# The last of 32 experts: its down piece in two column halves, its outputs added 32 rows at a time, another order of its products and transfers, and stores on two DMA queues

## The reference

```python
x = x + g1[:, None] * mix
h = rms_norm_2(x, norm2_g[l]) * (1.0 + sc2[:, None]) + sh2[:, None]
y = hierarchical_moe(h, w_rg, b_rg, w_re, b_re, w_gate, w_up, w_down)
x = x + g2[:, None] * y
return rms_norm_2(x, final_g)
```

## Time and profile before

| | |
|---|---|
| median of 3 runs | 916.79 us (915.58 to 919.57) |
| the profiled execution | 915.51 us |
| its span in the profile | 913.5 us |
| instructions | 13147 |
| busy share: PE, PE weight loads, DVE, ACT, POOL | 85%, 51%, 41%, 19%, 4% |
| moved from HBM | 282.75 MB |

### The profile page before, as it was taken

How to read it: one execution, slowest core, us unless ns; L and a number is a source line. 1 busy time by engine, 2 the same in 40 slices (tenths; PEclk the granted TensorE clock), 3 DMA queues, 4 the chain that set the end, 5 groups by cost and what they waited for, 6 DMA issues and landing times.

```text
span 913.5 us, 13147 instructions
## 1 busy us (share of the span) xinstructions
PE 773.8 (85%) x5441; PEld 466.3 (51%) x5441; DVE 373.0 (41%) x881; ACT 170.1 (19%) x473; POOL 39.6 (4%) x36
## 2 busy tenths in 40 slices
PE   7999899999998999998999996858767676677675
PEld 4544664456577644466477573535534444345332
DVE  2478678557854676537342322111111111121113
ACT  3222631213356310023120000000000000001001
POOL 1110000023300000000000000000000000000000
PEclk9999999999999999999999998999889999799779
DMA  9983507665003659972969999999999999999994
GB/s 344 395 310 130 185 1 272 235 231 184 1 1 134 224 159 379 396 298 77 382 254 411 426 427 429 428 429 429 428 428 429 427 430 429 427 430 429 424 430 174
DMA packets 54556, 284.40 MB, mean 311 GB/s; under 512 B 2800, under 2 KB 7280, under 8 KB 41968
## 3 DMA queue, kind: packets, MB, share of 16 engines
q1 hardware_dynamic: 54512, 283.81, 77.5%
HBM read 282.75 MB, written 1.05 MB: 311 GB/s over the span
## 4 chain that ended last, share of the span: by engine, by line
PE 57%; DMA 33%; DVE 4%; ACT 2%; issue 2%; POOL 1%; SPq 1%; DVEq 0%; POOLq 0%
DMA ring<-in_up_w 30%; PE banks L1800 15%; PE banks L1934 15%; PE banks L2298 8%; PE banks L1884 3%; DMA ring<-in_down_w 2%; PE banks L2346 2%; PE banks L1832 2%; PE banks L2283 2%; PE banks L1869 1%; PE banks L1912 1%; POOL rs L577 1%; PE banks L1778 1%; DVE soft L1070 1%; ACT probs L651 1%
## 5 line engine op out<-in xcount | busy, mean ns | idle before, releaser
L2298 PE MATMUL banks<-ring,QT 128*32 128x256 f32 x1696 | 143.8, 449 | 61.2 <-DMA ring<-in_up_w 61.2
L1934 PE MATMUL banks<-ring,hT 128*128 128x512 f32 (+4 forms) x384 | 157.2, 564 | 1.4 <-DMA ring<-in_ab_w 1.2
L1800 PE MATMUL banks<-ring,hT 128*128 128x512 f32 x320 | 139.9, 594 | 2.5 <-issue 1.5
L2298 PEld LDWEIGHTS banks<-ring,QT 128*32 128x32 f32 x1696 | 72.6, 124 | 110.1 <-DMA ring<-in_up_w 44.5
L1934 PEld LDWEIGHTS banks<-ring,hT 128*128 128x128 f32 x384 | 72.1, 192 | 74.3 <-issue 65.9
L1696 DVE TENSOR_TENSOR QT<-banks,MOD 32x256 f32<-32x256 f32 x128 | 53.8, 420 | 132.8 <-PE banks L2346 131.5
L1800 PEld LDWEIGHTS banks<-ring,hT 128*128 128x128 f32 x320 | 60.1, 190 | 78.9 <-issue 73.8
L1687 DVE TENSOR_TENSOR QT<-QT,banks 64x256 f32<-64x256 f32 x32 | 13.5, 423 | 195.2 <-ACT QT L919 195.2
L2346 PE MATMUL banks<-ring,QT 128*32 128x256 f32 x992 | 61.4, 387 | 14.9 <-ACT QT L926 12.4
L577 POOL TENSOR_TENSOR rs<-st,mhalf 128x1 f32<-128x1 f32 (+7 forms) x27 | 32.4, 1203 | 867.8 <-DVE st L1733 448.1
L919 ACT ACTIVATE QT<-banks 64x256 f32<-64x256 f32 x32 | 12.0, 375 | 292.2 <-PE banks L2298 292.2
(11 more groups left out here) (353 smaller groups left out, 712.8 us busy)
## 6 DMA issues: line engine op xcount, KB each, us to landing
ring<-in_up_w SPq DMA_DIRECT2D x30, 2048.0 KB, 23.7
ring<-in_down_w SPq DMA_DIRECT2D x30, 2048.0 KB, 21.9
ring<-in_gate_w SPq DMA_DIRECT2D x23, 2048.0 KB, 20.4
ring<-in_ada_w SPq DMA_DIRECT2D x12, 2048.0 KB, 15.3
probs<-in_gate_w SPq DMA_DIRECT2D x8, 2048.0 KB, 29.3
ring<-in_ab_w SPq DMA_DIRECT2D x4, 2048.0 KB, 19.8
ring<-in_cd_w SPq DMA_DIRECT2D x4, 2048.0 KB, 13.6
ring<-in_in_w SPq DMA_DIRECT2D x4, 2048.0 KB, 14.3
```

Of the source, the lines that this page charges most:

```text
L1800: ins = pe.matmul(bank[j % 4][:, 0:n], hT[:, k, t * P:(t + 1) * P], w[:, k, :], start=(k == 0), stop=(k == KD - 1))
L1934: ins = pe.matmul(bank[b][:, 0:n], hT[:, k, t * P:(t + 1) * P], w[:, k, :], start=(k == 0), stop=(k == KD - 1))
L2298: return pe.matmul(bank[1][CAP * j:CAP * j + CAP, 0:256], XG[:, k, CAP * s:CAP * s + CAP], wk[:, :, 2 * (j % 2):2 * (j % 2) + 2], start=(k ...
```

## The change

- **Transfers.** The loop runs on to the last expert, so the order becomes G30, U30, D30, G31, U31, D31. D31 comes in two halves of 512 columns (all four row chunks), each with its semaphore.
- **Order on TensorE.** Expert 31's gate_up follows down(30). Between its gate and its up products stand the additions of experts 28 to 30 (`add_outputs(7)` with 96 rows).
- **Down products of 31.** `down_last(half)`: for each column half 16 matmuls of 128 columns, in strips n = 0 to 3, into bank 0 or 1. Strip n gets columns 128n to 128n + 127 of the half. VectorE multiplies the 128x128 result once by the gate row, laid out in strips before (`outputs_last`, `gate_strips`).
- **Additions of 31.** `add_last(half)`: eight matmuls with 32 weight rows (one row strip each), 128 weight columns and 128 streamed ones, in two turns of four. A turn uses four row strips and four banks and waits for the turn before it. The weights are SW's last 32 columns, repeated four times and turned (`spread_last` at expert 24, two more transposes and a copy at 28).
- **Layout of the sums.** The banks of a token tile hold quarter columns: bank b has columns 256b to 256b + 255 of each half. Residual, additions and YE are read in that order.
- **The end.** ScalarE waits for all 16 sums and squares 128x1024 at once for each token tile; VectorE orders the two means and four row blocks by hand; SyncE stores column half 0 and ScalarE column half 1.

The diff, without the branch for crowded experts, which isn't run here:

```diff
+        def by_bank(a):
+
+            return a.rearrange("p (h b n) -> p b h n", h=2, b=2)
...
+        def sum_bank(t, b):
+            return bank[4 + 2 * t + b][:, :].rearrange("p (h n) -> p h n", h=2)
...
+        def sum_half(t, h):
+            return banks[:, 4 + 2 * t:6 + 2 * t, 256 * h:256 * h + 256]
...
+        gate_strips, last_out = [MOD[:, 1, 256 * i:256 * i + 256].rearrange("p (h n) -> p h n", h=2) for i in range(2)]
+        last_spread, last_spreadT = [MOD[:, 2, 256 * i:256 * i + 256].rearrange("p (t n) -> p t n", t=NT) for i in range(2)]
...
-                for e in range(6, NE - 2):
-                    for j in range(1 if e == 6 else 0, 3):
+                for e in range(6, NE):
+                    for j in range(1 if e == 6 else 0, 2 if e == NE - 1 else 3):
                         once_in_four = e % 2 == 0 and j == 0
                         load_gathered(3 * (e % 2) + j, e, e - 4 if once_in_four else e - 2)
-                for e in (NE - 2, NE - 1):
-                    for j in range(2):
-                        load_gathered(3 * (e % 2) + j, e, e - 4 if e % 2 == 0 and j == 0 else e - 2)
-                load_gathered(2, NE - 2, NE - 4)
                 sp.wait_ge(*upto("g_down", NE - 2))
                 down = srcs[2](NE - 1)
                 for half in range(2):
-                    sp.dma_start(ring[eslot(5)][:, 2048 * half:2048 * half + 2048].rearrange("p (k n) -> p k n", k=2),
-                                 down[:, 2 * half:2 * half + 2, :]).then_inc(sem(f"last_down{half}"), 16)
+                    sp.dma_start(ring[eslot(5)][:, 2048 * half:2048 * half + 2048].rearrange("p (k n) -> p k n", k=FC),
+                                 down[:, :, 512 * half:512 * half + 512]).then_inc(sem(f"last_down{half}"), 16)
...
-                for c in range(2):
-                    sp.wait_ge(*upto("out", 2 * t + c + 1))
-                    sp.dma_start(out[t * P:(t + 1) * P, 512 * c:512 * c + 512], X[:, t, 512 * c:512 * c + 512])\
-                      .then_inc(sem("st"), 16)
+                sp.wait_ge(*upto("out", 2 * t + 1))
+                store(sp, t, 0)
...
-                for b in range(4):
-                    act.wait_ge(*upto("sums", b + 1))
-                    sumsq(bank[4 + b][:, :], st[:, b:b + 1], "sum_ss", Y[:, b // 2, D + 512 * (b % 2):D + 512 * (b % 2) + 512])
+                act.wait_ge(*upto("sums", 16))
+                for t in range(NT):
+                    sumsq(banks[:, 4 + 2 * t:6 + 2 * t, :], st[:, t:t + 1], "sum_ss", in_halves(Y[:, t, D:2 * D]))
...
+            for t in range(NT):
+                act.wait_ge(*upto("out", 2 * t + 2))
+                store(act, t, 1)
...
+                if last_quad(q):
+                    v.tensor_copy(last_spreadT, bank[0][:, 256:512].rearrange("p (t n) -> p t n", t=NT))
...
+            def spread_last():
+
+                v.wait_ge(*upto("g_sw", QUADS))
+                v.tensor_copy(by_expert(last_spread), SW[:, :, 3 * CAP:4 * CAP].unsqueeze(2).to_broadcast([P, NT, 4, CAP]))\
+                 .then_inc(sem("g_swr"), 1)
+                for n in range(4):
+                    strip = slice(CAP * n, CAP * n + CAP)
+                    ins = v.tensor_copy(gate_strips[strip, :, :],
+                                        MOD[strip, 5, :].rearrange("p (h s n) -> p s h n", h=2, s=4)[:, n, :, :])
+                ins.then_inc(sem("g_swr"), 1)
+
+            def outputs_last(half):
+
+                v.wait_ge(*upto("g_down", NE + half))
+                if half == 0:
+                    v.wait_ge(*upto("g_swr", 2))
+                v.tensor_tensor(last_out[:, half, :], bank[half][:, 0:P], gate_strips[:, half, :], ALU.mult)\
+                 .then_inc(sem("g_ye"), 1)
 
...
-                    if e < NE - 1:
-                        hidden(e)
-                    if e == NE - 2:
-                        hidden(NE - 1)
+                    hidden(e)
                     if e % 4 == 0:
                         turned(q)
                         if q + 1 < QUADS:
                             select(q + 1)
                             spread(q + 1)
-                    outputs(e)
-                for t in range(NT):
-                    o = slice(2 * t, 2 * t + 1)
-                    v.wait_ge(*upto("sum_ss", 2 * t + 2))
-                    go(v.tensor_scalar(st2[:, t:t + 1], st[:, o], st[:, 2 * t + 1:2 * t + 2], D * EPS, ALU.add, ALU.add), "ms")
-                    rooted()
-                    for c in range(2):
-                        cols = slice(512 * c, 512 * c + 512)
-                        v.scalar_tensor_tensor(out=X[:, t, cols], in0=bank[4 + 2 * t + c][:, :], scalar=rs[:, t:t + 1],
-                                               in1=MOD[:, 0, cols], op0=ALU.mult, op1=ALU.mult).then_inc(sem("out"), 1)
+                        if q + 1 == QUADS - 1:
+                            spread_last()
+                    if e < NE - 1:
+                        outputs(e)
+                for half in range(2):
+                    outputs_last(half)
+
+                def final_mean(t):
+                    v.wait_ge(*upto("sum_ss", t + 1))
+                    means(1, 1.0, a=t, eps=D * EPS)
+
+                def final_rows(t, c):
+                    cols = slice(512 * c, 512 * c + 512)
+                    v.scalar_tensor_tensor(out=in_halves(X[:, t, cols]), in0=sum_half(t, c), scalar=rs[:, t:t + 1],
+                                           in1=in_halves(MOD[:, 0, cols]), op0=ALU.mult, op1=ALU.mult).then_inc(sem("out"), 1)
+
+                final_mean(0)
+                rooted()
+                final_rows(0, 0)
+                final_mean(1)
+                final_rows(0, 1)
+                rooted()
+                final_rows(1, 0)
+                final_rows(1, 1)
...
                             strip(k, j)
+                    add_outputs(q)
                     gathered_landed(pe, q, s, 1)
...
-                    gathered_landed(pe, q, s, 2)
+                gathered_landed(pe, q, s, 2)
                 pe.wait_ge(*upto("g_hc", e + 1))
                 if last_quad(q):
...
-                        pe.wait_ge(*upto(f"last_down{c // 2}", 16))
                     a = 64 * (c % 2) + CAP * (c // 2)
                     for n in range(4):
                         ins = pe.matmul(bank[2][CAP * n:CAP * n + CAP, 0:256], HG[:, a:a + CAP],
                                         wd(c)[:, 256 * n:256 * n + 256], start=(c == 0), stop=(c == FC - 1))
                 ins.then_inc(sem("g_down"), 1)
 
...
+            def down_last(half):
+
+                if half == 0:
+                    pe.wait_ge(*upto("g_hc", NE))
+                pe.wait_ge(*upto(f"last_down{half}", 16))
+                for c in range(FC):
+                    a = 64 * (c % 2) + CAP * (c // 2)
+                    at = 2048 * half + 512 * c
+                    for n in range(4):
+                        ins = pe.matmul(bank[half][CAP * n:CAP * n + CAP, 0:P], HG[:, a:a + CAP],
+                                        ring[eslot(5)][:, at + P * n:at + P * n + P], start=(c == 0), stop=(c == FC - 1))
+                ins.then_inc(sem("g_down"), 1)
+
+            def add_last(half):
+
+                pe.wait_ge(*upto("g_ye", NE + half))
+                for turn in range(2):
+                    if half + turn > 0:
+                        pe.wait_ge(*upto("sums", 8 * half + 4 * turn))
+                    for t in range(NT):
+                        for b in range(2):
+                            n = 2 * b + (t + turn) % 2
+                            strip = slice(CAP * n, CAP * n + CAP)
+                            at = 256 * half + P * (n % 2)
+                            pe.matmul(bank[4 + 2 * t + b][:, at:at + P], last_spreadT[strip, t, :], last_out[strip, half, :],
+                                      start=False, stop=half + turn == 2, tile_position=(CAP * n, 0)).then_inc(sem("sums"), 1)
+
...
+                if last_quad(q):
+                    pe.wait_ge(*upto("g_swr", 1))
+                    for t in range(NT):
+                        ins = pe.transpose(bank[0][:, 2 * P + P * t:3 * P + P * t], last_spread[:, t, :], ident)
                 ins.then_inc(sem("g_swt"), 1)
...
-            def add_outputs(q, last=False):
-
+            def add_outputs(q):
+
+                experts = 3 if last_quad(q) else 4
+                some = slice(0, CAP * experts)
                 pe.wait_ge(*upto("g_swc", q + 1))
-                pe.wait_ge(*upto("g_ye", q * 4 + 4))
+                pe.wait_ge(*upto("g_ye", q * 4 + experts))
                 for j in range(4):
-                    ins = pe.matmul(bank[4 + j][:, :], SWT[:, j // 2, :], YE[:, 512 * (j % 2):512 * (j % 2) + 512],
-                                    start=False, stop=last)
-                    if last:
-                        ins.then_inc(sem("sums"), 1)
-                if not last:
```

(15 more changed lines are left out.)

## The result

The changed kernel takes 920.31 us (median of 20 runs, 918.88 to 922.98), the kernel before 917.47 (20 runs, 915.44 to 921.5). The ratio is 1.0029, with a 95% interval of 1.002 to 1.0039: slower by 2.8 us, too little to pass the 0.5% set in the prediction. Forecast were 2.8 us and "about the same". The profiled executions lie further apart, 919.84 and 915.51; e5 to e11 show a part of why.

What follows compares the result with a forecast made beforehand. Expert weight transfers bound the kernel until about 880, so the last 33 us decide. Additions +1.1 and a longer end +1.7 gave +2.8 us, put on the median 916.79: 919.6 us, range 916.0 to 922.5.

Steps and rivals of the forecast that it cites:

- the 0.5% set in the prediction: Whole kernel: smallest difference told from no change, about 0.5% or 4.6 us, from runs reaching 915.58 to 919.57.
- The transfers: Last weight pieces: expert 30's down lands 885.6, expert 31's gate 890.4, up 895.3, down 899.9 including 0.4 for 2 KB runs.
- Up to the hidden rows: Expert 31 on TensorE: gates from 890.8, 3.3 us; additions 3.67, 2.5 on the path; up 3.3, ending 901.1.
- Down products and turns: Expert 31: down halves 0.93 us each, then four turns of 32-row additions at 0.72 each; last sum 908.0, +1.1 us.
- the second rival: Expert 31's additions: row strips don't overlap, a turn costs 1.3 us, total 921.9; decides from about 1.2; chance 0.15.
- The rule of the Trainium skill on serialized increments: Expert 31's additions: increments on every packed matmul serialize, 26.3 ns each, an estimated 0.4 us more, 920.0 in the end.
- The factor for four row strips: Expert 31's additions: four row strips at 3.07 times one, an estimated 0.6 us a turn, 0.5 us less in all.
- The end: Squares, means and row blocks: last sum to last row 5.2 us, 1.7 more than 3.5, as all banks close together.
- The store: After the last rows: last store lands 3.07 us later, kept from before, as each last store has a free queue.
- Additions at no cost: Rival at expert 31's up products: set by the up piece's landing alone, all after 2.5 us earlier, 917.1; chance 0.15.
- An order that doesn't show: Rival on transfers: expert 30's down piece lands one piece late, 890.4, its products 1.6 us later, 921.2; chance 0.05.
- A gain: Whole kernel: faster by more than 4.6 us; nothing reaches it, as up can't end before 898.6; chance 0.05.

Runs made afterwards that it cites:

- e5: The kernel before, unchanged, traced once more for its scatter: 916.63 us, last rows to end 3.06 us.
- e11: The kernel before, unchanged, for a third trace of the granted clock: last rows to end 2.5 us, clock 0.51 in the last additions; no total time given.
- e1: Changed kernel with the additions of experts 28 to 30 between gate and up of expert 31 left out: ratio 1.0006, median 918.11 us.
- e2: Changed kernel with the additions of experts 28 to 30 moved behind expert 31's down products, ahead of the 32-row additions: ratio 1.0049.
- e7: Kernel before with only the new end (squares of 128x1024 after all sums, new order of means and row blocks), one queue: ratio 1.0027.
- e3: Changed kernel with all four stores on SyncE's queue again: ratio 1.005.
- e6: Kernel before with column half 1 stored from ScalarE's queue and nothing else: ratio 1.0014.
- e4: Changed kernel with the earlier order of transfers and products, additions of experts 28 to 30 behind the down halves: ratio 1.0027.
- e9: Kernel before with ten idle matmuls on TensorE in the waits before expert 31's down products and the last additions: ratio 0.9994, median 917.06 us.
- e8: Kernel before with earlier additions of experts 28 and 29, outputs of 30 and 31 added in strips, new end, two queues: ratio 1.001.
- e10: The kernel before with strip additions for experts 30 and 31 and the new end, but all stores on SyncE's queue: ratio 0.9986, median 915.64 us.

## Why the prediction came out

**The transfers.** Right in order and time: gates at 891.07 for 890.4 (the stream was 0.7 late as a whole), down(30) without a wait. D31 landed at 901.17 for 899.9. The 0.4 us for its 2 KB runs was near: it lands 5.1 to 5.2 us after the piece ahead of it in the five kernels with column halves, 4.9 in the eight with row halves, so 0.2 to 0.3. Of the 1.3 us that it came later than forecast, 0.7 is the later stream, and 0.7 comes from taking the end of the bytes, 899.5, for the landing, 900.18. All of it stayed hidden here, as the products came at 904.38.

**Up to the hidden rows.** The mechanism is shown by e1 and e2. Two terms were mis-sized: gates and up were each put at half of 6.58, 3.3 us; apart they take 3.82 and 3.77, because each is a full run of its own and nothing of one runs beside the other. Before, the last of the gates and the first of the ups ran side by side: 18 records are at work between 891.1 and 891.9, 10 between 889.6 and 890.4. So splitting them costs 1.0 us in itself, whatever stands between. With the gates' start 0.4 late, up ends at 902.43 for 901.1.

**Down products and turns.** Halves 1.96 together for 1.86; four turns 2.6 us for 2.9. The row strips overlap; the second rival is out, since it needed 1.2 us a turn and the longest was 0.62. The rule of the Trainium skill on serialized increments ("TensorE: Matmul & The Clock Gate", "The cost: per-tile semaphore tail") has no 0.4 us to show here: all four turns came out below the sum without it. No run leaves the increments out, so the rule itself isn't tested. The factor for four row strips in the Trainium skill (same page, "Measured speedup vs the span model") fits better: the estimate from it was 0.6 a turn, and the trace agrees, with 0.55 to 0.62.

**The end.** 4.88 us from last sum to last row for 5.2, against 3.52; e7 shows the 1.4 alone. The store was the term that failed: 3.07 was kept, the trace has 4.2. Neither the queue (e3, e6) nor the bunching (e7) explains it alone. The five traces of the changed kernel and e1 to e4 show 4.05 to 4.2, the six of the kernel before, e6, e7 and e9 2.5 to 3.1, and e8 and e10 3.6 and 3.7. The DMA view has something that goes with these three groups: a 16 KB packet of queue 8, "instruction". The changed kernel from 912.5 on, and the kernel before from 909.1 on, each from 1.3 us ahead of the end of the last rows to the end (GB/s in 40 slices):

```profile
GB/s 104 432 328 417 313 268 298 343 506 357 343 313 343 387 328 372 373 402 357 372 402 120 30 60 45 45 15 30 30 15 30 30 0 0 0 0 0 0 0 0
...
q8 instruction: 1, 0.02, 1.1%
q14 instruction: 1, 0.01, 0.4%
```

```profile
GB/s 112 0 19 0 37 19 149 335 391 391 391 354 298 131 410 317 372 354 354 372 391 391 391 372 391 391 205 0 19 19 37 19 19 0 0 0 0 0 0 0
...
q14 instruction: 1, 0.01, 0.7%
```

In the changed kernel that packet begins at 913.73, among the last stores, and takes 0.93 us; behind the bulk of the bytes come about 1.4 us at 15 to 60 GB/s. In the kernel before the last such packet is over at 908.95, and that tail is 0.7 us. So it is in all 13 traces: in the five with 4.05 to 4.2 us the packet is still under way when the last rows end, by 0.3 to 0.9 us; in e8 and e10 it is over 0.2 and 0.7 us ahead of that, in the other six at least 1.4. This is a coincidence in time, and the likeliest cause; no run moved the packet, so it isn't shown.

**The other rivals.** Additions at no cost: out, by e1. An order that doesn't show: out, D30 was there at 888.78. A gain: none.

**What the agreement is worth.** By the two spans the change costs 4.5 us. The sum missed 0.4 for a later stream, 1.0 at gate and up and 1.1 at the store, and had 0.7 too much in turns and end. It met the medians because the trace of before was a good execution, 2.0 us under its median of 20 (the one after 0.5 under). The mechanism was right, but that the number agrees so closely is luck. Two things make such executions differ. One is the granted clock: in three of five traces the last additions took 1.7 us longer. The other is the stream: U30 landed between 880.2 and 883.1 in the eight traces of the kernel before and its edits, 880.3 and 884.1 in the other five, so the 0.7 of a later stream lies within the scatter. With the clock the changed kernel may save something that neither the prediction nor its rows had, as its TensorE has no wait of 1.9 us before its last matmuls. That isn't shown: by e9, doing without idle waits is worth anything between nothing and 1.9 us.

## What to carry to other kernels

When the last transfers of a stream stand one piece apart, moving one forward moves the others back by the same length; what hung on these must then have something to hide in, and filling their wait with other work helps only as long as that work is no longer than the wait. Two sets of products on separate column strips can overlap where they meet; once something stands between them each costs its full time, so a split is priced at two whole runs (3.8 us each here) and not at two halves of the joint one (3.3). A sum at the scale of a few us should be set against several executions of the kernel before: a single trace can be 2 us better than the median. And the end of a transfer's bytes is not its landing: what hangs on a piece is set against the row of its first user.

## What the hardware showed that was not expected

- The granted clock fell to 0.50 (1.2 GHz) in the last few us in some executions and not in others of the same work: the last additions took 5.4 us in place of 3.67 in three of five traces.
- Gate products on two column strips alone took 3.82 us for 32 records, as did up; both in one sequence took 6.58, not 7.6.
- Four row strips of 32 weight rows and 128 columns each ran a turn of eight records in 0.55 to 0.62 us, and of 256 columns in about 0.8, with a wait for the turn before in it.
- An issue of a store on SyncE took between 0.33 and 1.33 us in the same program (e3). In the 13 traces, each of the seven store issues longer than 0.6 us began while a 16 KB instruction packet was under way; some others that did took 0.34.
- The last bytes of D31 move by 899.5 in the kernel before, and it lands at 900.18.
